# Block products over half their depth for both row tiles, with weight buffers released and refilled by halves

## The reference

```
def swiglu_ffn(x, w_gate, w_up, w_down):
    return (jax.nn.silu(x @ w_gate) * (x @ w_up)) @ w_down
...
x = x + 0.5 * swiglu_ffn(rmsnorm(x, ffn1_norm[l]), ffn1_w_gate[l], ffn1_w_up[l], ffn1_w_down[l])
```

## Time and profile before

| | |
|---|---|
| median of 3 runs | 1778.1 us (1777.47 to 1778.37) |
| the profiled execution's own time | 1777.71 us |
| its span, first to last instruction | 1775.9 us |
| mean granted TensorE clock | 0.995 |
| busy: PE / DVE / ACT | 1721.1 / 1010.5 / 704.5 us |
| chain that ended last | PE 85%, DVE 9%, ACT 5%, issue 1% |
| ffn1 sets / ffn2 sets | about 938 to 1206 us / about 1466 to 1734 us |

### The profile page before, as it was taken

How to read it: one execution, slowest core, us unless ns; L and a number is a source line. 1 busy time by engine, 2 the same in 40 slices (tenths; PEclk the granted TensorE clock), 3 DMA queues, 4 the chain that set the end, 5 groups by cost and what they waited for, 6 DMA issues and landing times.

```text
span 1775.9 us, 21351 instructions
## 1 busy us (share of the span) xinstructions
PE 1721.1 (97%) x8703; PEld 1277.9 (72%) x8703; DVE 1010.5 (57%) x1489; ACT 704.5 (40%) x1144; POOL 78.9 (4%) x78
## 2 busy tenths in 40 slices
PE   7999999998999999999999999999999999999998
PEld 6878888885454545454477788898877887788896
DVE  4768865643333333333457866765577457856765
ACT  4556435441111111111335445454355435545453
POOL 0000000000000000000001111100000001111100
PEclk9999999998999999999999999999999999999999
DMA  6222225547999999999947888883303167898781
GB/s 216 94 72 72 95 81 180 193 154 289 421 421 420 421 421 421 420 421 421 372 122 170 213 201 196 179 190 124 119 0 107 49 194 185 192 220 196 166 200 56
DMA packets 117512, 385.74 MB, mean 217 GB/s; under 512 B 7088, under 2 KB 22592, under 8 KB 91424
## 3 DMA queue, kind: packets, MB, share of 16 engines
q1 hardware_dynamic: 88928, 318.33, 46.7%
q0 software_dynamic: 26176, 61.78, 18.9%
q10 hardware_dynamic: 2304, 4.20, 0.6%
HBM read 364.36 MB, written 6.29 MB: 209 GB/s over the span
## 4 chain that ended last, share of the span: by engine, by line
PE 85%; DVE 9%; ACT 5%; issue 1%; DMA 0%; SPq 0%; DVEq 0%; ACTq 0%
PE PS L1491 12%; PE PS L1600 8%; PE PS L1602 8%; PE PS L1601 8%; PE PS L1524 6%; PE PS L1630 6%; PE PS L1632 6%; PE PS L1631 6%; PE PS L1634 3%; PE PS L1636 3%; PE PS L1635 3%; DVE lo L2386 2%; PE PS L1462 2%; PE PS L1463 2%; PE PS L1534 2%; PE PS L1708 2%
## 5 line engine op out<-in xcount | busy, mean ns | idle before, releaser
L2386 DVE TENSOR_TENSOR lo<-raw,hi 128x1024 fp32r<-128x1024 f32 (+2 forms) x273 | 328.1, 1232 | 199.1 <-ACT hi L1939 195.6
L1939 ACT CAST hi<-raw 128x1024 fp32r<-128x1024 f32 (+2 forms) x275 | 282.4, 1066 | 220.9 <-PE PS L1602 142.9
L1600 PE MATMUL PS<-hi,xh_ffn 128*128 128x512 f32 (+1 forms) x320 | 118.5, 370 | 6.3 <-issue 4.0
L1602 PE MATMUL PS<-hi,xl_ffn 128*128 128x512 f32 (+1 forms) x320 | 117.6, 368 | 0.0
L1601 PE MATMUL PS<-lo,xh_ffn 128*128 128x512 f32 (+1 forms) x320 | 117.5, 367 | 0.0
L1491 PE MATMUL PS<-raw,XG 128*64 128x512 f32 x352 | 117.1, 593 | 0.0
L2346 DVE TENSOR_TENSOR HF<-SG,PS 128x512 f32<-128x512 f32 x16 | 17.4, 1090 | 164.8 <-PE PS L1491 164.8
L2361 DVE SCALAR_TENSOR_TENSOR YL<-PS,SM,YH 128x512 fp32r<-128x512 f32 x30 | 21.1, 746 | 138.8 <-ACT YH L1922 138.8
L2369 DVE TENSOR_TENSOR x_sb<-x_sb,PS 128x512 f32<-128x512 f32 x128 | 78.2, 678 | 8.7 <-PE PS L1535 8.7
L1905 ACT COPY HT<-PS 128x512 f32<-128x512 f32 x16 | 9.4, 586 | 175.1 <-PE PS L1500 175.1
L1634 PE MATMUL PS<-xTh,hi 128*128 128x512 f32 x192 | 78.3, 408 | 0.4 <-DVE lo L2386 0.3
(11 more groups left out here) (520 smaller groups left out, 4237.5 us busy)
## 6 DMA issues: line engine op xcount, KB each, us to landing
raw<-in_w_in SPq DMA_DIRECT2D x26, 1024.0 KB, 5.1
rawz<-in_w_down_experts SPq DMA_DIRECT2D x25, 1024.0 KB, 10.9
raw<-in_w_up_experts SPq DMA_DIRECT2D x24, 1024.0 KB, 16.0
raw<-in_w_gate_experts SPq DMA_DIRECT2D x20, 1024.0 KB, 15.5
raw<-in_ffn_w_down SPq DMA_DIRECT2D x20, 1024.0 KB, 6.0
rawz<-in_w_up_experts SPq DMA_DIRECT2D x19, 1024.0 KB, 19.1
raw<-in_w_down_experts SPq DMA_DIRECT2D x16, 1024.0 KB, 12.0
rawz<-in_w_gate_experts SPq DMA_DIRECT2D x16, 1024.0 KB, 13.8
```

The lines of the kernel that those rows point to most:

```text
L1600: e.matmul(o, xh[:, k, c], h[:, k, :], start=k == 0 and not more, stop=False, skip_group_check=more)
L1602: x = e.matmul(o, xl[:, k, c], h[:, k, :], start=False, stop=k == 3, skip_group_check=more)
L1939: e.copy(q.hi[:, a:b], q.raw[:, a:b]).then_inc(*a_hi((u, 0) if part == 0 else u))
L2386: e.tensor_tensor(q.lo[:, a:b], q.raw[:, a:b], q.hi[:, a:b].bitcast(F32), ALU.subtract).then_inc(*v_lo(key))
```

## The change

A product's two row tiles are run together: two depth blocks for t = 0, the same two for t = 1, then the other two blocks for each. PE waits for the first halves of `hi` and `lo` before the product and for the second halves in its middle. It signals once in the middle (after the first two depth blocks of both tiles) and at the end of each tile. The first half of the unit for product j+2 waits for that middle signal of product j (`hl_first`), if it is no wider; the second half waits for the end, as before. In the list of steps the first half of product j+2 (`hi`, then `lo`) stands right behind product j, ahead of `behind[j]`; its second half stands where `take` of product j+1 puts it. Which matmuls, roundings, evictions and DMAs there are, and their sizes, is unchanged but for the first such unit of a network, whose `hi` and `lo` are now made in halves.

```diff
     def split_to(self, j):
         while self.split < min(j, len(self.units)):
-            if self.halves and self.units[self.split].four:
+            if self.units[self.split].four:
                 u = self.first + self.split
-                self.steps.extend([("hi", u, 0), ("hi", u, 1), ("lo", u, 0), ("lo", u, 1)])
+                if self.rounded:
+                    self.steps.extend([("hi", u, 1), ("lo", u, 1)])
+                else:
+                    self.steps.extend([("hi", u, 0), ("hi", u, 1), ("lo", u, 0), ("lo", u, 1)])
                 self.split += 1
+                self.rounded = False
                 continue
...
+    def split_first(self):
+        u = self.first + self.split
+        if self.split < len(self.units) and self.units[self.split].four:
+            self.steps.extend([("hi", u, 0), ("lo", u, 0)])
+            self.rounded = True
...
             u = feed.take((pre, *what))
             S.extend(ahead if j == 0 else ())
-            S.extend(("seven", (pre, *what), j, t, u) for t in range(2))
+            S.append(("seven", (pre, *what), j, u))
+            feed.split_first()
             S.extend(behind[j])
...
                 u.hl_free = at_hl[j] if j < len(at_hl) else [U[first + j - 2].done]
+                if j >= len(at_hl) and U[first + j - 2].half and u.n <= U[first + j - 2].n:
+                    u.hl_first = [U[first + j - 2].half]
...
+                for half in range(2):
+                    pe.wait_ge(a_hi, u if half else (u, 0))
+                    pe.wait_ge(v_lo, u if half else (u, 0))
+                    for t in range(2):
+                        b = BANK[j] + t
+                        if not half:
+                            if not more:
+                                taken(b)
+                            elif key[1] == "s":
+                                pe.wait_ge(v_sum, ("x", key[0], key[2], PAST[j], t))
...
+                        for k in (2 * half, 2 * half + 1):
...
+                        if half:
+                            x.then_inc(*p_mm((key, j, t)))
+                        elif t:
+                            x.then_inc(*p_mm((key, j, "half")))
...
-                for s, k in q.hl_free:
+                for s, k in q.hl_first if part == 0 and q.hl_first else q.hl_free:
                     act.wait_ge(s, k)
                 e.copy(q.hi[:, a:b], q.raw[:, a:b]).then_inc(*a_hi((u, 0) if part == 0 else u))
```

More of the change, by code:

```diff
@@ L115, in __init__ @@
         self.key, self.src, self.kc, self.n = key, src, kc, n
-        self.raw = self.hi = self.lo = self.slot = self.done = self.made = self.four = None
+        self.raw = self.hi = self.lo = self.slot = self.done = self.half = self.made = self.four = None
         self.last = False
         self.raw_free, self.hl_free, self.lo_free = [], [], []
+        self.hl_first = None
 class Feed:
@@ L126, in __init__ @@
         self.split = self.taken = 0
-        self.spread, self.rounded, self.halves = False, False, False
+        self.spread, self.rounded = False, False
     def split_hi(self):
@@ L682, in schedule_ffn @@
     past = None
-    feed.halves = True
     for what in SETS:
@@ L1152, in place @@
                 u.hl_free = at_hl[h] if j < len(his) else [U[first + j - len(his)].done]
+        for f in fours.values():
+            for j, q in enumerate(f.plan):
+                q.half = (p_mm, (f.key, j, "half"))
         for group, first, n in ((p1, 0, len(p1)), (p2, first_moe, len(p2)), (p3, first3, len(p3)), (p5, first5, len(p5))):
@@ L1412, in first_sum, with seven @@
                 onto(f.t3, f.b22.src, "T3", f)
-            def seven(key, j, t, u):
+            def seven(key, j, u):
                 f = fours[key]
                 nxt = SETS.index(key[1:]) + 1
-                if t:
-                    return
                 if j == 0:
@@ L1578, in turn_hidden, with seven @@
                 freed[b] = [(v_ev, ("h", n, p, cut, tb))] if p == NS else [(a_ev, ("hT", n, p, cut, tb))]
-            def seven(key, j, t, u):
+            def seven(key, j, u):
                 q = U[u]
-                b = BANK[j] + t
                 h, l = (x[:, 0:4 * q.n].rearrange("p (k n) -> p k n", k=4) for x in (q.hi, q.lo))
                 xh, xl = (LEFT_H if key[1] == "s" else LEFT_X)[j]
-                pe.wait_ge(a_hi, u)
-                pe.wait_ge(v_lo, u)
                 more = j in PAST
[L1588 to L1595, removed]
-                left_ready(pe, key, j)
[L1597 to L1607, removed]
@@ new lines, in seven @@
+                left_ready(pe, key, j)
+                for half in range(2):
[8 more added lines that the diff above has]
+                                pe.wait_ge(v_sum, ("x", key[0], key[2], PAST[j], t))
+                            elif j == 6:
+                                pe.wait_ge(v_ev, ("C22", *at_set(key), t))
+                            else:
+                                pe.wait_ge(a_ev, ({3: "R1", 4: "R2", 5: "R4"}[j], *at_set(key), t))
+                        c = slice(t * 128, t * 128 + 128)
+                        o = PS[:, b, 0:q.n]
+                        for k in (2 * half, 2 * half + 1):
+                            e.matmul(o, xh[:, k, c], h[:, k, :], start=k == 0 and not more, stop=False, skip_group_check=more)
+                            e.matmul(o, xh[:, k, c], l[:, k, :], start=False, stop=False, skip_group_check=more)
+                            x = e.matmul(o, xl[:, k, c], h[:, k, :], start=False, stop=k == 3, skip_group_check=more)
+                        if half:
+                            x.then_inc(*p_mm((key, j, t)))
+                        elif t:
+                            x.then_inc(*p_mm((key, j, "half")))
@@ L1609, in mm @@
+                for t in range(2):
+                    b = BANK[j] + t
+                    if key[1] == "s":
+                        freed[b] = [(v_sum, ("x", key[0], key[2], j, t))]
+                    elif j in (2, 5, 6):
+                        freed[b] = [(v_ev, ({2: "C11", 5: "ht", 6: "C21"}[j], *at_set(key), t))]
             def mm(key, ui, i, u, a=0, b=None):
```

## The result

The changed kernel took 1802.8 us, median of 4 runs (1801.4 to 1805.3), against 1777.8 us for the kernel before on the same chip: 1.0143 times as long, 95% interval 1.0125 to 1.0160, or 25.0 us more. The forecast was 1801. The profiled execution took 1801.43 us and is the shortest of the four.

The account below looks back on a forecast made before the run. TensorE bounds the kernel, with VectorE's in-order queue setting the "s" set stalls. 22.3 - 4.6 + 5.6 = +23.3 us on 1777.7 gave 1801 us, range 1787 to 1812.

Parts of the forecast that it names:

- The "s" sets: Four sets of block products in ffn1 and ffn2: evictions queue behind waiting half roundings, +5.6 us per set, bounds +2.5 and +8.
- The four stalls: TensorE waits in "s" sets before products 4, 5, 6 and the next set: 3.6, 1.8, 1.1 and 0.6 us.
- The term of +22.3 us: Loss of all four "s" sets together, +5.6 us each, containing the loss of the two old stalls.
- The first sets: First set of each network: old stalls go, bank 4 comes 1 us late; net -3.6 us in ffn1, -1.0 in ffn2.
- the 1.51 us: Old stall before product 0 of ffn1's first set; goes because `lo` in halves is ready at about 936.5.
- The other sets: Late `hb` in (1,1), (2,1), 0.8 us each; ACT queue in (1,0), (2,0), (2,1), 0.4 each; +5.6 us over both networks.
- the stall of (1,1): Before product 4 of set (1,1): R2 copy on ACT arrives as late as before, so no gain from the 1.14 us.
- rival C: Slower: 3.6 us stall before product 4 halves TensorE's clock, 2 us in each of four "s" sets, 1809 us; 14%.
- Rival A: Faster: halves fill free time, all 14 stalls go, 1758 us; decided by L2500 starting before 5.4 us into product 4; 6%.
- B: About no change: "s" backlog absorbed, +1 per "s" set instead of +5.6, 1783 us or less; 10%.
- D: Half release does nothing, first halves wait for whole products, all chains grow by 2.72 us, over 1820 us; 2%.
- No term for the DMAs: DMA issues on SP and POOL keep their conditions and loads start no later, so nothing was added for them.

Follow-up runs that it names:

- the first experiment: Changed kernel with first halves for product j+2 moved behind `behind[j]`, product order, half waits and early release kept: 1773.2 us, ratio to before 0.9974.

## Why the prediction was right

**The "s" sets.** The chain that the prediction worked out against what the first of them did: product 1 at 7.15 us (7.06), product 3 at 18.1 (18.05), product 4 at 27.2 (27.14); then 7.28 (7.26), 6.66 (6.56), 6.13 (6.18); in sum 47.3 (47.14). ACT's half `hi` starts 3.07 us after the product, predicted 3.09. The four stalls were 3.47, 1.56, 0.87 and 0.43, predicted 3.6, 1.8, 1.1 and 0.6. The term of +22.3 us came out at 24.45 - 4.47 = 20.0 without the clock. It was sized on the first "s" set for all four; the second of each network is followed by units of 384 columns, whose first half takes VectorE 0.96 us, and its last two steps are shorter (5.70 us to the next set, where the first has 6.18): 46.3 us with its slow matmuls taken out.

**The cause** is shown, not only fitted: with the first halves behind the evictions the loss is gone (1773.2), with the "s" sets alone put back 24.9 us go, and with `lo` alone moved behind, the chain still shows through ACT.

**The first sets.** -4.6 predicted (ffn1 3.6, ffn2 1.0), -4.8 measured (3.5 and 1.3). That the gain comes from starting on half a unit is shown by the runs with half waits (1773.0) and without (1777.1). The prediction gave the 1.51 us to the first unit's `lo` in halves, and of it 0.97 went in the run that starts no product on half a unit.

**The other sets.** +5.6 predicted, +5.9 measured, set by set: (1,1) +0.8 (predicted 0.8), (1,0) and (2,0) +0.5 (0.4), (2,1) +1.2 (1.2). The places are the predicted ones: product 1 of (1,1) comes 7.07 us after the set's start instead of 6.34, and in (1,0) product 4 comes 5.69 after product 3 instead of 5.44. That the stall of (1,1) stays was right, and I got the same stall wrong in the expectation of the first experiment, for the kernel whose ACT order is otherwise the old one: its cause is the rounding of S3, which is there in either order.

**The clock, rival C,** happened in part and in addition: three of four stalls were followed by slow matmuls, 1.3 to 1.6 us each, 4.5 us in all, not 2 in each of four. Its place and its mechanism were right, with a chance of 14% for the full effect, and its sign, a granted clock under 1.00 behind the stalls, appeared. The forecast carried nothing for it. That the profiled execution hit 1801 all the same is luck: the "s" sets were 2.3 us oversized, and 1.8 us went ahead of ffn1 in that execution. The two executions of 1804.1 and 1805.3 us have a mean granted clock of 0.991 and 0.990 where the profiled one has 0.993, so in those more of the time was slow. The Trainium skill, "TensorE: Matmul & The Clock Gate", "Part 1: The HAM clock gate", ties the lower clock to TensorE having been idle and the return to activity. The rows above agree in kind: 0.58 behind 3.48 us of idle time in the second "s" set, and 1.00 again behind the next stall.

**The range.** Its lower end, 1787, is 1789 by the prediction's own terms (1777.7 + 4 x 2.5 - 4.6 + 5.6); nothing hangs on it.

**Rival A** fell where it was said to be decided: the evictions of product 4 (L2522) start at 1010.38, 6.4 us after the product does, not before 5.4. **B** fell with the backlog, which nothing absorbed. **D** fell on 3.07 us.

**No term for the DMAs** held: no wait of a block product names one. Landing times after the change were not measured by themselves.

## What to carry to other kernels

An engine's queue is in order, so an instruction that is moved ahead has to be ready no later than what it overtakes: giving a buffer back earlier is worth nothing if the instruction that uses it waits in front of the evictions that the same product needs. Split the wait first (here 4 us for a product that starts on half of its operand) and leave the order of the steps alone. Of a stall in a backlog ask which of two causes comes last: here mending the evictions' place or the late product alone gave 0.1 us or less per "s" set, and both edits together 0.8.

## What of the hardware was not expected

The granted clock fell after less idle time than I had thought, and not surely. TensorE's stalls of 2.33 to 2.35 us were followed by slow matmuls in three of four cases, those of 3.47 and 3.48 us in three of four, and those of 4.60 us in all four; the 50 stalls of 1.28 to 1.75 us that the twelve profiles show in the sets, in none. Equal stalls differ: 2.33 us before 1544.79 kept 1.00 where 2.34 us before 1004.50 left 0.58. What tells them apart is open, and idle time in one piece is not all of it: at the router of the first block, ahead of everything that was changed, TensorE waits 1.23 us before 384.2 us and then runs short matmuls of 36 and 128 columns for 2.7 us, and in eight of the twelve profiles the granted clock fell there (0.59 between 386 and 390 us in the kernel before), in four it stayed at 1.00 (the kernel after among them). Two executions differ by 1.4 us by that alone. In the "s" sets the price was 1.2 to 1.6 us behind 2.3 and 3.5 us of idle time and 1.6 to 2.5 us behind 4.6, so that a stall behind which the clock falls costs about one and a half times its length.
